# One block for the first stage, and a second level of picks over 64 candidate pairs

## The reference

```
mod = silu(c) @ w_ada + b_ada            # 1024 -> 6 x 1024: shift1, scale1, gate1, ...
h = x / sqrt(mean(x*x) + eps) * norm1_w * (1 + scale1) + shift1
```

```
top_s, top_i = top_k(s, 16)                            # per head and half
cand_s = top_s[half 0][:, None] + top_s[half 1][None, :]    # 16 x 16 sums
best_s, best_pos = top_k(cand_s, 16)
idx = top_i[half 0] * 128 + top_i[half 1] at best_pos
gate = softmax(best_s)
out = sum over picks of gate * gelu(h . u[idx]) * v[idx]
```

## Time and profile before

| | us |
|---|---|
| median of 3 runs (3722.16 to 3733.29) | 3729.78 |
| the profiled execution | 3702.43 |
| its span, first to last instruction | 3700.6 |
| end of the first stage, start of the first projection | 66.2, 67.2 |
| tile 0's picks, first half, to the index | 321.5 to 350.9 |
| tile 0's second half and tile 1's picks, with steps between | 354.1 to 492.5 |
| picks of tiles 2 and 3, with steps between | 858.4 to 1069 |

### The profile page before, as it was taken

How to read it: one execution, slowest core, us unless ns; L and a number is a source line. 1 busy time by engine, 2 the same in 40 slices (tenths; PEclk the granted TensorE clock), 3 DMA queues, 4 the chain that set the end, 5 groups by cost and what they waited for, 6 DMA issues and landing times. The chain is left out here.

```text
span 3700.6 us, 44636 instructions
## 1 busy us (share of the span) xinstructions
PE 2746.5 (74%) x17746; PEld 1979.5 (53%) x17746; DVE 2136.4 (58%) x3975; ACT 592.3 (16%) x1229; POOL 1311.7 (35%) x1082
## 2 busy tenths in 40 slices
PE   5977553678880086889885757799999789777777
PEld 4866443464330075677773636478888667322232
DVE  6544999878748977968777988424222453200001
ACT  1021002200000012122212310132222330100001
POOL 0001366666767765757655566300000000000000
PEclk7988776788995587889987778999999889899998
DMA  7616588888999988889979699622333324899997
GB/s 273 229 40 222 198 293 317 299 326 328 329 343 370 376 310 302 312 309 369 356 259 362 219 336 363 227 91 87 101 101 96 117 80 172 331 428 428 428 429 321
DMA packets 390749, 1006.30 MB, mean 272 GB/s; under 512 B 30381, under 2 KB 234515, under 8 KB 375699
## 3 DMA queue, kind: packets, MB, share of 16 engines
q0 software_dynamic: 150912, 549.52, 40.0%
q1 hardware_dynamic: 211856, 406.65, 29.9%
q10 hardware_dynamic: 27779, 47.38, 3.5%
HBM read 971.99 MB, written 31.46 MB: 271 GB/s over the span
## 5 line engine op out<-in xcount | busy, mean ns | idle before, releaser
L1496 POOL DMA_INDIRECT ring<-in_peer_u_dram,index x512 | 685.0, 1338 | 448.0 <-DVE ring L1574 240.4
L1496 POOL DMA_INDIRECT ring<-in_peer_v_dram,index x512 | 597.4, 1167 | 334.6 <-DVE h_rows_b L1580 144.6
L345 PE MATMUL bank<-hT,weights 128*128 128x256 f32 x1984 | 459.3, 396 | 144.5 <-ACTq L142 72.3
L345 PEld LDWEIGHTS bank<-hT,weights 128*128 128x128 f32 x1984 | 394.6, 200 | 208.6 <-issue 130.0
L1891 PE MATMUL bank<-hT,weights 128*128 128x256 f32 x1792 | 431.2, 396 | 6.5 <-DVE weights L2089 4.1
L1891 PEld LDWEIGHTS bank<-hT,weights 128*128 128x128 f32 x1792 | 343.2, 196 | 60.9 <-DVE weights L2089 4.5
L1574 DVE SCALAR_TENSOR_TENSOR ring<-ring,h_rows_a 128x1024 f32<-128x1024 f32 x256 | 305.1, 1223 | 60.4 <-DMA ring<-in_peer_u_dram,index 56.4
L1580 DVE SCALAR_TENSOR_TENSOR h_rows_b<-ring,coef,h_rows_b 128x1024 f32<-128x1024 f32 x238 | 305.2, 1283 | 43.3 <-DMA ring<-in_peer_v_dram,index 23.2
L1574 DVE SCALAR_TENSOR_TENSOR ring<-ring,h_rows_b 128x1024 f32<-128x1024 f32 x256 | 299.4, 1223 | 4.4 <-DMA ring<-in_peer_u_dram,index 4.0
L2908 POOL IOTA mo_down<- 128x4 f32 x1 | 0.1, 144 | 792.5 <-POOLq L160 792.5
L1593 PE MATMUL bank<-ring,weights 128*128 128x512 f32 x512 | 227.4, 606 | 20.6 <-DVE weights L1568 13.7
(11 more groups left out here) (570 smaller groups left out, 4290.8 us busy)
## 6 DMA issues: line engine op xcount, KB each, us to landing
weights<-in_w_in_dram SPq DMA_DIRECT2D x112, 512.0 KB, 3.8
weights<-in_w_in_dram SPq DMA_DIRECT2D x54, 1024.0 KB
xp_near<-in_w_exp_gate_dram SPq DMA_DIRECT2D x9, 4096.0 KB, 34.3
xp_far<-in_w_exp_up_dram SPq DMA_DIRECT2D x9, 4096.0 KB, 33.2
xp_near<-in_w_exp_up_dram SPq DMA_DIRECT2D x7, 4096.0 KB, 33.9
xp_far<-in_w_exp_gate_dram SPq DMA_DIRECT2D x7, 4096.0 KB, 35.7
xp_near<-in_w_exp_down_dram SPq DMA_DIRECT2D x7, 4096.0 KB, 34.4
xp_far<-in_w_exp_down_dram SPq DMA_DIRECT2D x7, 4096.0 KB, 34.4
```

What stands on the lines that cost most here:

```text
L345: ins = pe.matmul(m.ps[b][:, 0:TH], m.weights[:, s, k, c * P:(c + 1) * P], rhs(k), start=(k == 0), stop=(k == k_tiles - 1))
L1496: pool.indirect_dma_start(out=self.ring[:, n % RING, :], out_offset=None, in_=self.tables[table], in_offset=bass.IndirectOffsetOnAxis(ap=s ...
```

## The change

In the first stage the two Blocks are one. The first set of columns has a semaphore of its own and is turned and kept first, before x; the other three sets are turned behind the last copy of xT. ScalarE copies xT out of the banks, in turn with its squares. SP issues all eight slices of w_ada before the four of w_in. VectorE builds the masks, keeps the first columns and begins with the steps; it takes the mean ahead of step 6 and inverts one half of the root ahead of step 7 and the other behind it. The product with the root no longer has scale1 in it and is made before mod is known; scale and shift are applied afterwards in one instruction a slice, the even slices on VectorE, the odd ones on ScalarE.

In the picks the pair of ranks (a, b) is only a candidate if b is below a width that falls with a: 16 for a = 0, 8 for 1 to 3, 4 for 4 to 7, 1 for 8 to 15. That makes 64 a head in place of 256. A place among the 64 is turned back into a rank a by comparing it with the places where each rank begins (`begin`) and adding up the rises of the first index between the ranks up to it (`rise`), and into a rank b by masking the place with 15, 7, 3 or 0.

```diff
     def load(self, eng):
         for i, rows in enumerate(self.sets):
             for key, ap in rows:
                 r = self.at[i][key]
-                eng.dma_start(self.raw[r:r + ap.shape[0], i, :], ap).then_inc(self.landed, 16)
-
-    def turn(self, pe, bank):
-        pe.wait_ge(self.landed, 16 * sum(len(rows) for rows in self.sets))
-        for i, cols in enumerate(self.cols):
-            n = cols.shape[1]
+                eng.dma_start(self.raw[r:r + ap.shape[0], i, :], ap).then_inc(self.landed[min(i, 1)], 16)
+
+    def part(self, j):
+        return range(1, len(self.sets)) if j else range(1)
...
+    def turn(self, pe, j, bank):
+        pe.wait_ge(self.landed[j], 16 * sum(len(self.sets[i]) for i in self.part(j)))
+        for i in self.part(j):
+            n = self.cols[i].shape[1]
             ins = pe.transpose(bank[:, i * P:i * P + n], self.raw[0:n, i, :], self.m.ident[0:n, 0:n])
         ins.then_inc(self.turned, 1)
...
+    def keep(self, dve, j, bank):
+        dve.wait_ge(self.turned, j + 1)
+        for i in self.part(j):
+            cols = self.cols[i]
+            ins = dve.tensor_copy(cols[:, :], bank[:, i * P:i * P + cols.shape[1]])
+        ins.then_inc(self.kept, 1)
...
+    def scales_made(self, dve):
+        self.m.dve.wait(dve)
+        dve.sem_inc(self.scaled, 1)
+
+    def apply(self, eng, h, odd):
+        m = self.m
+        if odd:
+            eng.wait_ge(self.scaled, 1)
+        for k in range(odd, KT, 2):
+            if odd:
+                eng.activation(h[:, k, :], h[:, k, :], ACT.Identity, bias=m.mod[:, k:k + 1], scale=m.scale1[:, k:k + 1])
+            else:
+                eng.tensor_scalar(h[:, k, :], h[:, k, :], m.scale1[:, k:k + 1], m.mod[:, k:k + 1], ALU.mult, ALU.add)
...
         @block.sync
         def _(sp):
             sp.dma_start(rows[:, :, :], x.rearrange("(t p) d -> p t d", p=P)).then_inc(landed, 16)
-            for n in range(ada.BUFS):
+            for n in range(KT):
                 ada.load(sp, n)
-
-        @block.scalar
-        def _(act):
-            columns.load(act)
+            prefetch(m, sp, *then)
+            for n in range(KT, KT + ada.BUFS):
+                ada.load(sp, n)
...
         @block.tensor
         def _(pe):
+            columns.turn(pe, 0, first_bank)
             pe.wait_ge(landed, 16)
             for k in range(KT):
+                if k == KT - 1:
+                    pe.wait_ge(columns.kept, 1)
                 for t in range(TT):
                     ins = pe.transpose(m.ps[k][:, t * P:(t + 1) * P], rows[:, t, k * P:(k + 1) * P], m.ident[:, :])
                 ins.then_inc(turned, 1)
-            pe.wait_ge(kept, 1)
-            columns.turn(pe, m.ps[0])
+            pe.wait_ge(kept, KT)
+            columns.turn(pe, 1, rest_bank)
+            for k in range(KT):
+                pe.wait_ge(squared, k + 1)
+                ins = pe.matmul(sum_bank[:, :], m.ones[:, :], m.hT[:, k, :], start=(k == 0), stop=(k == KT - 1))
+            ins.then_inc(rooted, 1)
+            ada.sum_up(pe, mod_bank, 0, 1)
+
+        @block.scalar
+        def _(act):
+            columns.load(act)
+            act.wait_ge(columns.kept, 1)
+            act.activation(m.silu_c[:, :], ada.cols[:, at["c"]:at["c"] + KT], ACT.Silu).then_inc(silu_made, 1)
+            for k in range(KT):
+                act.wait_ge(turned, k + 1)
+                act.copy(m.xT[:, k, :], m.ps[k][:, :]).then_inc(kept, 1)
+                if k:
+                    act.wait_ge(kept, k)
+                    act.activation(m.hT[:, k - 1, :], m.xT[:, k - 1, :], ACT.Square).then_inc(squared, 1)
+            act.wait_ge(kept, KT)
+            act.activation(m.hT[:, KT - 1, :], m.xT[:, KT - 1, :], ACT.Square).then_inc(squared, 1)
+            act.wait_ge(rooted, 2)
+            act.activation(rstd[:, :], rstd[:, :], ACT.Sqrt).then_inc(rooted, 1)
+            ada.apply(act, m.hT, 1)
...
         @block.vector
         def _(dve):
+            c = m.dve
             m.pool.wait(dve)
             levels.build(dve)
             masks.build(dve)
-            m.dve.mark(dve.memset(carry.shift[:, :, :], 0.0))
-            m.dve.mark(dve.memset(carry.halo[:, 0], 0.0))
-            for k in range(KT):
-                dve.wait_ge(turned, k + 1)
-                dve.tensor_copy(m.xT[:, k, :], m.ps[k][:, :]).then_inc(kept, 1)
-            columns.keep(dve, m.ps[0])
-
-    silu_made, squared, rooted = m.sem("silu_made"), m.sem("x_squared"), m.sem("x_rooted")
-    scaled = m.sem("x_scaled")
-    rstd = own.enter_context(nc.sbuf_tensor("x_rstd", [P, T], F32))
-    at = ada.at
-    with nc.Block() as block:
-
-        @block.sync
-        def _(sp):
-            prefetch(m, sp, *then)
-            for n in range(ada.BUFS, KT + ada.BUFS):
-                ada.load(sp, n)
-
-        @block.scalar
-        def _(act):
-            act.activation(m.silu_c[:, :], ada.cols[:, at["c"]:at["c"] + KT], ACT.Silu).then_inc(silu_made, 1)
-            for k in range(KT):
-                act.activation(m.hT[:, k, :], m.xT[:, k, :], ACT.Square).then_inc(squared, 1)
-            act.wait_ge(rooted, 2)
-            act.activation(rstd[:, :], rstd[:, :], ACT.Sqrt).then_inc(rooted, 1)
-            for k in range(KT):
-                act.wait_ge(scaled, k + 1)
-                m.act.mark(act.activation(m.hT[:, k, :], m.hT[:, k, :], ACT.Identity, bias=m.mod[:, k:k + 1]))
-
-        @block.tensor
-        def _(pe):
-            for k in range(KT):
-                pe.wait_ge(squared, k + 1)
-                ins = pe.matmul(m.ps[1][:, :], m.ones[:, :], m.hT[:, k, :], start=(k == 0), stop=(k == KT - 1))
-            ins.then_inc(rooted, 1)
-            ada.sum_up(pe, m.ps[0], 0, 1)
-
-        @block.vector
-        def _(dve):
+            columns.keep(dve, 0, first_bank)
+            c.mark(dve.memset(carry.shift[:, :, :], 0.0))
+            c.mark(dve.memset(carry.halo[:, 0], 0.0))
             dve.wait_ge(silu_made, 1)
             for n in range(KT):
-                if n == KT // 2:
+                if n == 6:
                     dve.wait_ge(rooted, 1)
-                    dve.tensor_scalar(rstd[:, :], m.ps[1][:, :], 1.0 / D, EPS, ALU.mult, ALU.add).then_inc(rooted, 1)
+                    dve.tensor_scalar(rstd[:, :], sum_bank[:, :], 1.0 / D, EPS, ALU.mult, ALU.add).then_inc(rooted, 1)
+                    columns.keep(dve, 1, rest_bank)
+                if n == 7:
+                    dve.wait_ge(rooted, 3)
+                    c.mark(dve.reciprocal(rstd[:, 0:TH], rstd[:, 0:TH]))
                 ada.add(dve, n)
-            dve.wait_ge(rooted, 3)
-            m.dve.link(dve, dve.reciprocal(rstd[:, :], rstd[:, :]))
-            ada.keep(dve, m.ps[0], 0, 1)
-            m.dve.wait(dve)
+            c.link(dve, dve.reciprocal(rstd[:, TH:T], rstd[:, TH:T]))
+            dve.wait_ge(kept, KT)
             for k in range(KT):
-                dve.scalar_tensor_tensor(out=m.hT[:, k, :], in0=m.xT[:, k, :], scalar=m.scale1[:, k:k + 1],
-                                         in1=rstd[:, :], op0=ALU.mult, op1=ALU.mult).then_inc(scaled, 1)
+                c.mark(dve.tensor_tensor(m.hT[:, k, :], m.xT[:, k, :], rstd[:, :], ALU.mult))
+            ada.keep(dve, mod_bank, 0, 1)
+            ada.scales_made(dve)
+            ada.apply(dve, m.hT, 0)
...
+BANDS = ((0, 1, 16), (1, 4, 8), (4, 8, 4), (8, 16, 1))
+STARTS = tuple(sum(b * (min(r, a1) - a0) for a0, a1, b in BANDS if r > a0) for r in range(TOPK + 1))
+CANDS = STARTS[TOPK]
...
-        self.cand = one.rearrange("p (h n) -> p h n", h=PH)
-        self.cand2 = two.rearrange("p (h n) -> p h n", h=PH)
+        self.cand = one.rearrange("p (h n) -> p h n", h=PH)[:, :, 0:CANDS]
+        self.cand2 = two.rearrange("p (h n) -> p h n", h=PH)[:, :, 0:CANDS]
...
+        for a0, a1, width in BANDS:
+            m.pool.mark(pool.iota(self.begin[:, a0:a1], [[width, a1 - a0]], base=STARTS[a0], channel_multiplier=0,
+                                  allow_small_or_imprecise_dtypes=True))
...
+        steps, table, kind = ((self.begin, self.rise[:, h, :], ALU.is_le), (self.count, i4[:, h, 1, :], ALU.is_equal))[j]
         if step == 0:
-            c.link(dve, dve.tensor_tensor(w3, self.count[:, :].unsqueeze(1).to_broadcast([P, H * TOPK, TOPK]),
-                                          self.digitf[:, j, picks].unsqueeze(2).to_broadcast([P, H * TOPK, TOPK]),
-                                          ALU.is_equal))
+            c.link(dve, dve.tensor_tensor(w3, steps[:, :].unsqueeze(1).to_broadcast([P, H * TOPK, TOPK]),
+                                          self.digitf[:, j, picks].unsqueeze(2).to_broadcast([P, H * TOPK, TOPK]), kind))
         elif step == 1:
-            c.link(dve, dve.tensor_tensor(which, which, i4[:, h, j, :].unsqueeze(2).to_broadcast([P, H, TOPK, TOPK]), ALU.mult))
+            c.link(dve, dve.tensor_tensor(which, which, table.unsqueeze(2).to_broadcast([P, H, TOPK, TOPK]), ALU.mult))
         else:
```

(28 more changed lines are left out.)

20 lines of the change are left out of this document (12 added, 8 removed).

## The result

The changed kernel takes 3697.51 us (median of 7 runs) where the kernel before takes 3716.19 on the same chip (7 runs): a ratio of 0.9938, 95% interval 0.9914 to 0.9962. The ratio is not that of the two medians, which lie 18.7 us apart; here it agrees with that of the means, which lie 23 us apart. The profiled execution is the median one, 3697.5, with a span of 3695.7.

What follows compares the result with a forecast made beforehand. No engine was taken to bound the whole (TensorE 74% busy, VectorE 58%), so each stretch had its own limit. Savings of 14.2 + 2.0 + 3.0 + 7.3 = 26.5 us took the median 3729.8 to 3703, range 3686 to 3719.

Steps and rivals of the forecast that it cites:

- First stage: Start of the kernel up to the first projection: it would end at 52 in place of 66.2, saving 14.2 us.
- Table load, hidden: ScalarE's load of the silu table in the first stage: 1.28 us hidden in a wait, otherwise costing 1.3 us.
- Early half of tile 0: Tile 0's first half of picks, which frees the first gather: between 0 and 3.0 us saved, taken as 2.0.
- Late half: Tile 0's second half of picks, in the stretch that VectorE limits: its 3.0 us saving counts in full.
- tile 1: Tile 1's picks, in the stretch before 510 that VectorE limits: the 7.3 us saving counts in full.
- rival 1: Gathers set the pace before 510 too, so pick savings become waits for rows; 3715.6 us, chance 0.12.
- Tiles 2 and 3: Picks of these tiles, 863 to 1108: the 14.6 us saved on VectorE count nothing, since TensorE covers them.
- Rival 4: Slower through instruction supply in the picks: gaps of 9.3 us each, from the fourth on slower, 3740; chance 0.06.
- Sum: Whole kernel: first stage 14.2, tile 0's picks 2.0 and 3.0, tile 1's 7.3, together 26.5 us saved.

Runs made afterwards that it cites:

- e1: Kernel before with only the first stage's part of the change, picks as before: 3609.29 us, ratio 0.9952 to the kernel before.
- e5: Changed kernel with TensorE's sums of squares put ahead of the turn of the other three column sets: 3683.74 us, ratio 0.9902 to the kernel before.
- e10: Changed kernel with sums of squares before the other columns, six early gathers for twelve, exponentials behind the thirteenth query copy: 3679.97 us, ratio 0.9896 to before.
- e2: Kernel before with only the picks' part of the change, first stage as before: 3614.73 us, ratio 0.9968 to the kernel before.
- e7: Changed kernel with six of the twelve early gathers issued in tile 0's query Block, the rest behind it: 3679.94 us, ratio 0.9896 to before.
- e11: Changed kernel with sums of squares before the other columns, three early gathers for twelve, exponentials behind the thirteenth query copy: 3686.1 us, ratio 0.992 to before.
- e4: Kernel before once more, unchanged, for a second profile: 3623.08 us, ratio 0.9995 to the kernel before.
- e3: Changed kernel once more, unchanged, for a second profile: 3590.22 us, ratio 0.9907 to the kernel before.
- e9: Changed kernel a third time, unchanged, on another chip: 3701.09 us against 3721.82, ratio 0.9936 to the kernel before.
- e8: Changed kernel with the 256-wide second level of picks restored in tiles 2 and 3 only: 3705.23 us, ratio 0.9942 to the kernel before.

## Why the prediction held, step by step

- **First stage, 14.2 forecast, 14.8 measured** (13.8 in e1). The first nine loads were in by 12.7, not 14, but what the steps waited for was VectorE's masks, to 14.4, so step 0 began at 14.97 (15.3). The forecast's own terms, 15 us of transfers from 5.5, put slice 3 at 20.5 and not at 22; the trace has it at 23.0. Last step 40.9 (41.6), sum-up to 47.9 (48.7), projection 52.3 (53). Step 6 waited 3.4 (2.8). TensorE's sums took 9.46 us where I had 8.66. The clock granted in the window 24 to 28 was 0.50, the 1.2 GHz level, after TensorE had stood still for most of the four microseconds ahead; e5 ran the same sixteen products straight behind the transposes in 7.03. The Trainium skill (DMA: Bandwidth & Descriptors, "Queues, rings and completion order") says that each DMA engine serves its queues in turn: the trace agrees, with nine small loads in at 12.7 while SP's megabytes kept the engines at a share of 1.03.
- **Table load, hidden.** It ran at 12.61, ahead of its wait. One exposed case is in e10: a copy ends at 321.75, the load runs 1.28 from 321.77, the exponential starts at 323.07. That is 1.32 us in all; no drain beyond it is to be seen. The Trainium skill (ScalarE: Activation LUTs, "Step-by-step: what each stage is for") gives about 2.7 us including the drain; the measured 1.32 decides.
- **Early half of tile 0, 2.0 forecast: this step failed, with a small term.** It was worth -1.0 (15.1 at 320, 14.1 at the restart), and -0.9 in e2. The forecast had put the block's end behind the first gather plus 15 us of transfers, and took 1.0 off the 3.0 for the weights slice that now lies among them. The transfers do decide (e7, e11), but they no longer ran full from the start, and that cost 4 and not 1. A window of before and one of after, 2.8 and 1.1 us behind the first gather's issue:

```profile
354.00:358.00 4.00, 1.30 (x12) 1.11 (x10) 3.85 (x28) 1.30 (x3) 3.08 (x4) 1.00 1.04 399
```

```profile
334.00:338.00 4.00, 4.00 (x34) 3.90 (x34) 1.08 (x4) 2.35 (x4) 2.81 (x3) 1.00 0.63 195
```

Before, the last megabyte of w_in was issued just ahead of the gathers and filled the engines while these started; with the index 3.3 us earlier it comes in the middle. (In before the share is already 1.09 from 352 to 354, 0.8 us behind that issue.) From the index to the end of the last gather's last packet 7.3 MB took 19.8 us in before and 24.0 in after. That is so wherever the picks are the old ones (e1 19.8, e4 19.9) and wherever they are new with twelve gathers (e2 24.0, e3 23.5, e9 24.3), so the 4 us come with the picks and not with a chip or an execution. That it is the place of w_in's last megabyte that eats them is read from the windows and was not tried by itself.

- **Late half 3.0 and tile 1 7.3: 10.3 forecast, 10.9 measured** (10.8 in e2): 3.2 to 400, 1.1 to 440, 6.6 to 465. In full, as forecast, for GpSimd's last wait for VectorE came at 485.4 (484): rival 1 falls.
- **Tiles 2 and 3, nothing: right**, with VectorE 16.4 us less busy and the lead 24.4 before, 22.6 after; e8 shows it from the other side.
- **Rival 4** did not happen up to 1440: no gap of its size cost lead. From 1500 to 1900, where none of the changed instructions are, TensorE's time put down to issue is 35.6 us in after against 29.9 in before. Such gaps come on some chips and not on others, in before too; what causes them, want of instructions or something else, no run shows.
- Sum: 26.5 forecast, 25.0 by the trace at 491. The three ratios give 23, 24 and 34 us; the last one's interval, 25 to 43, reaches down to it. That the median 3697.5 lies so near the forecast 3703 is in part luck: the three runs in the forecast's table stood 13.6 us above the median of all seven, and the gain by the medians was 18.7 us where the forecast had 27. What is shown is the place of the gain in the traces up to 491, step by step.

## What to carry to other kernels

A start-up stage is judged by its DMA queue: find the windows in which the transfers stand still although megabytes are due, and ask which small wait holds the slots; then ask whether a full queue carries what is needed first. The early semaphore and the order of the loads each kept some 6 of the 14.8 us without the other. Where all engines meet at a Block's end behind a burst of prefetches, the burst's transfers can hold the restart, and an earlier start of the burst need not buy anything (here 3.3 us earlier bought none); put off the part that isn't needed, here six of twelve gathers for 7 us. A shorter chain on an engine pays only in the stretch in which someone waits for it: 10.9 us of the saved VectorE time counted, and 16 did not.

## What the runs showed of the hardware

- The kernel before took 3623 us in one group of runs and 3716 to 3722 in the others, on other chips, 2.6% more. Between a profile of each the difference is 0.5 us at 820, 27 at 1107, 28 at 1440 and 80 at 1990, and then grows no more. In that part the slower chip's DMA engines move 334 GB/s against 370 to 375, and TensorE's stream has gaps of about 1 us from 1500 to 1900 that the faster chip does not have. Which of these is cause is not shown.
- After the burst of gathers no engine begins the next Block before the transfers are through: with twelve, six and three gathers the restart followed the end of their last packet by 2.3 to 2.4, 2.0 to 2.2 and 2.0 us, in 14 profiles.
- MAX8, FIND_INDEX8 and MATCH_REPLACE8 on 64 elements take 213, 225 and 220 ns, in line with 289 ns for MAX8 on 128 in the same trace.
